# The last chunk of h turned by way of memory, in three stages of an encoder block

## The reference, cut to what matters

```python
h = h + 0.5 * swiglu(rmsnorm(h, ffn1_norm), ffn1_w_in, ffn1_w_out)
z = rmsnorm(h, mix_norm) @ w_mix_in
y = concat([rmsnorm(gating_unit(z), gnorm_a), rmsnorm(attention(z), gnorm_b)])
h = h + y @ w_mix_out
h = h + memory_cross_attention(rmsnorm(h, cross_norm), rmsnorm(mem, mem_norm), w_cq, w_ckv, w_co)
h = h + 0.5 * swiglu(rmsnorm(h, ffn2_norm), ffn2_w_in, ffn2_w_out)
out = rmsnorm(h, final_norm)
```

## Time and profile before

| | us |
|---|---|
| median of 3 runs (2161.65 to 2161.88) | 2161.73 |
| the profiled execution's own time | 2162.15 |
| its span | 2159.7 |
| PE (matmul) busy | 2149.6, 100% |
| DVE busy | 1167.4, 54% |
| ACT busy | 990.9, 46% |

### The profile page before, as it was taken

How to read it: one execution, slowest core, us unless ns; L and a number is a source line. 1 busy time by engine, 2 the same in 40 slices (tenths; PEclk the granted TensorE clock), 3 DMA queues, 4 the chain that set the end, 5 groups by cost and what they waited for, 6 DMA issues and landing times.

```text
span 2159.7 us, 26579 instructions
## 1 busy us (share of the span) xinstructions
PE 2149.6 (100%) x9544; PEld 1782.2 (83%) x9544; DVE 1167.4 (54%) x1158; ACT 990.9 (46%) x1133; POOL 46.2 (2%) x49
## 2 busy tenths in 40 slices
PE   9999999999999999999999999999999999999998
PEld 7888888888888888888888888888888888888887
DVE  5555555554555475556555644565555555554444
ACT  6444444443444455455444543454444444444443
POOL 0000000000000050000000000000000000000000
PEclk9999999999999999999999999999999999999999
DMA  8766676666666666765587765576666666765554
GB/s 302 248 218 212 213 225 218 213 214 193 217 224 213 244 230 218 246 216 172 173 288 236 230 205 185 183 226 210 213 225 218 213 214 222 220 213 193 193 186 155
DMA packets 179987, 466.05 MB, mean 216 GB/s; under 512 B 16721, under 2 KB 65105, under 8 KB 179793
## 3 DMA queue, kind: packets, MB, share of 16 engines
q1 hardware_dynamic: 177760, 457.90, 65.6%
q0 software_dynamic: 1728, 6.82, 0.9%
q10 hardware_dynamic: 432, 0.45, 0.1%
HBM read 438.36 MB, written 26.74 MB: 215 GB/s over the span
## 4 chain that ended last, share of the span: by engine, by line
PE 99%; DMA 1%; issue 0%; DVE 0%; ACT 0%; SPq 0%; POOL 0%; POOLq 0%; DVEq 0%; ACTq 0%
PE acc L1419 32%; PE acc L1421 32%; PE acc L1422 32%; PE acc L1517 1%; PE aux L1673 1%; PE aux L1653 1%; DMA bounce<-stage 0%; DMA memq<-bounce 0%; PE aux L1509 0%; PE aux L1610 0%; PE aux L1600 0%; PE aux L1573 0%; PE tp L1436 0%; PE acc L1496 0%; PE acc L1494 0%
## 5 line engine op out<-in xcount | busy, mean ns | idle before, releaser
L905 DVE TENSOR_TENSOR w_lo<-raw,w_hi 128x1024 fp32r<-128x1024 f32 x767 | 939.0, 1228 | 939.9 <-ACT w_hi L550 938.0
L550 ACT ACTIVATE w_hi<-raw 128x1024 fp32r<-128x1024 f32 x767 | 810.4, 1060 | 1092.1 <-PE acc L1422 1073.9
L1419 PE MATMUL acc<-w_hi,a_hi 128*128 128x512 f32 x1384 | 540.8, 391 | 0.0
L1422 PE MATMUL acc<-w_hi,a_lo 128*128 128x512 f32 x1384 | 539.3, 390 | 0.0
L1421 PE MATMUL acc<-w_lo,a_hi 128*128 128x512 f32 x1384 | 539.2, 390 | 0.0
L1419 PE MATMUL acc<-w_hi,b_hi 128*128 128x512 f32 x1216 | 476.5, 392 | 0.0
L1422 PE MATMUL acc<-w_hi,b_lo 128*128 128x512 f32 x1216 | 473.9, 390 | 0.0
L1421 PE MATMUL acc<-w_lo,b_hi 128*128 128x512 f32 x1216 | 473.9, 390 | 0.0
L1419 PEld LDWEIGHTS acc<-w_hi,a_hi 128*128 128x128 f32 x1384 | 260.0, 188 | 55.0 <-issue 1.3
L1422 PEld LDWEIGHTS acc<-w_hi,a_lo 128*128 128x128 f32 x1384 | 260.0, 188 | 53.8
L1421 PEld LDWEIGHTS acc<-w_lo,a_hi 128*128 128x128 f32 x1384 | 260.0, 188 | 53.3
(11 more groups left out here) (147 smaller groups left out, 623.9 us busy)
## 6 DMA issues: line engine op xcount, KB each, us to landing
raw<-in_ffn_w_in SPq DMA_DIRECT2D x351, 512.0 KB, 4.2
raw<-in_ffn_w_out SPq DMA_DIRECT2D x176, 512.0 KB, 4.3
raw<-in_w_mix_in SPq DMA_DIRECT2D x80, 512.0 KB, 4.3
raw<-in_w_ckv SPq DMA_DIRECT2D x64, 512.0 KB, 4.2
memq<-bounce SPq DMA_DIRECT2D x188, 128.0 KB, 3.7
bounce<-stage SPq DMA_DIRECT2D x37, 512.0 KB, 5.0
raw<-in_w_mix_out SPq DMA_DIRECT2D x32, 512.0 KB, 4.4
raw<-in_w_cq SPq DMA_DIRECT2D x32, 512.0 KB, 3.9
```

What stands on the lines that cost most here:

```text
L550: eng.activation(w_hi[:, u % RING], raw[:, u % RING], ACT.Copy).then_inc(w_hi_done, 1)
L905: eng.tensor_tensor(w_lo[:, u % RING], raw[:, u % RING], w_hi[:, u % RING].bitcast(f32), ALU.subtract).then_inc(w_lo_done, 1)
L1419: eng.matmul(dst, x_hi[:, rows], w_hi[:, slot, i], start=start and i == 0, stop=False)
L1422: last = eng.matmul(dst, x_lo[:, rows], w_hi[:, slot, i], start=False, stop=stop and i == UK - 1)
```

## The change

The last chunk of h goes by memory too, in all three places. PE's transposes, t_full, PE_FILLS, fill and fill_h are gone. SP sends the chunk ahead of load 7 of the next stage's first chunk and fetches it ahead of the second load of the chunk after (loads 7 and 8 stand between; the one that follows the fetch is load 9, counted from the first chunk's start). DVE turns it behind the split of unit 6 and subtracts behind that of unit 7; ACT's fill_hi stands behind its split of unit 7 and waits for the turn (turned) in place of t_full. mean_square comes ahead of the turn in all three. POOL's load_mem(0) waits for the new turn. On the host the rows of the last 512 of w_mix_in, w_cq, ffn2_w_in and the three gains are reordered as well.

```diff
@@ TURNS @@
-PE_FILLS = [("h1", 1), ("h2", 1), ("h3", 1)]
-TURNS = [("hid1", FJ), ("h1", DC - 1), ("qk", 4), ...
-         ("ck1", 1), ("yb1", 1), ("ck2", 1), ("ck3", 1), ("h2", DC - 1)] + ...
-         ("h3", DC - 1), ("hid2", FJ)]
+TURNS = [("hid1", FJ), ("h1", DC), ("qk", 4), ...
+         ("ck1", 1), ("yb1", 1), ("ck2", 1), ("ck3", 1), ("h2", DC)] + ...
+         ("h3", DC), ("hid2", FJ)]
@@ sync @@
-            def chunk(w, index, base, after_long=False, late=None, early=None, first=False):
+            def chunk(w, index, base, after_long=False, late=None, early=None, first=False, last=None,
+                      before=None):
                 for u in range(U8):
...
+                    if last and u == U8 - 1:
+                        send(*last)
+                    if before and u == 1:
+                        fetch(before[0])
                     load(w, index + u, base, u, after_long)
...
-                    chunk(w, 0, base, late=late)
-                    chunk(w, U8, base + U8)
+                    chunk(w, 0, base, late=late, last=last)
+                    chunk(w, U8, base + U8, before=last)
...
-                chunk(w_mix_in, U8 * c, MIX_IN + U8 * c, after_long=c == 0, late=late)
+                chunk(w_mix_in, U8 * c, MIX_IN + U8 * c, after_long=c == 0, late=late,
+                      last=from_h("h1", DC - 1) if c == 0 else None,
+                      before=from_h("h1", DC - 1) if c == 1 else None)
...
+                      last=from_h("h2", DC - 1) if c == 0 else None,
+                      before=from_h("h2", DC - 1) if c == 1 else None)
...
-            ffn_in(ffn2_w_in, FFN2_IN, "hid2", late=from_h("h3", DC - 2))
+            ffn_in(ffn2_w_in, FFN2_IN, "hid2", late=from_h("h3", DC - 2), last=from_h("h3", DC - 1))
@@ gpsimd @@
-            eng.wait_ge(turned, number(TURNS, "h1", DC - 2) + 1)
+            eng.wait_ge(turned, number(TURNS, "h1", DC - 1) + 1)
             load_mem(0)
@@ scalar @@
-                    if u == 6 and c == 0:
-                        fill_hi(t_full, number(PE_FILLS, "h1") + 1, a_hi[:, 3 * 4:4 * 4],
+                    if u == 7 and c == 0:
+                        fill_hi(turned, number(TURNS, "h1", 3) + 1, a_hi[:, 3 * 4:4 * 4],
                                 GAIN_AT["mix_norm"] + 3 * 4)
...
-                    if u == 6:
-                        fill_hi(t_full, number(PE_FILLS, "h3") + 1, b_hi[:, 12:16], GAIN_AT["ffn2_norm"] + 12)
+                    if u == 7:
+                        turned_h3_hi(DC - 1)
@@ vector @@
                     if u == 6 and c == 0:
                         mean_square("h1", DC, D)
+                        turn_fill("h1", DC - 1, number(TURNS, "h1", DC - 1))
+                    if u == 7 and c == 0:
                         fill_lo(split_number("h1", 3), a_lo[:, 12:16], a_hi[:, 12:16],
                                 GAIN_AT["mix_norm"] + 12)
...
                     if u == 6:
+                        mean_square("h3", DC, D)
+                        turn_fill("h3", DC - 1, number(TURNS, "h3", DC - 1))
+                    if u == 7:
                         fill_lo(split_number("h3", 3), b_lo[:, 12:16], b_hi[:, 12:16],
                                 GAIN_AT["ffn2_norm"] + 12)
-                        mean_square("h3", DC, D)
@@ tensor @@
-            def fill(srcs):
...
-                for k in range(4):
-                    for t in range(NT):
-                        last = eng.transpose(tp[:, k, t * P:(t + 1) * P], srcs(k, t), ident[:])
-                last.then_inc(t_full, 1)
...
-                    if u == 2 and c == 0:
-                        fill_h("h1", "h1", DC - 1)
...
-                    if u == 2 and c == 0:
-                        fill_h("h2", "h2", DC - 1)
...
-                    if u == 2:
-                        fill_h("h3", "h3", DC - 1)
```

More of the change, by code:

```diff
@@ L46 @@
          ("h2", DC), ("h3", DC), ("hid2", FJ)]
-PE_FILLS = [("h1", 1), ("h2", 1), ("h3", 1)]
-TURNS = [("hid1", FJ), ("h1", DC - 1), ("qk", 4), ("ya0", 1), ("ya1", 1), ("ck0", 1), ("yb0", 1),
-         ("ck1", 1), ("yb1", 1), ("ck2", 1), ("ck3", 1), ("h2", DC - 1)] + [(f"cq{k}", 1) for k in range(DC)] + [
-         ("h3", DC - 1), ("hid2", FJ)]
+TURNS = [("hid1", FJ), ("h1", DC), ("qk", 4), ("ya0", 1), ("ya1", 1), ("ck0", 1), ("yb0", 1),
+         ("ck1", 1), ("yb1", 1), ("ck2", 1), ("ck3", 1), ("h2", DC)] + [(f"cq{k}", 1) for k in range(DC)] + [
+         ("h3", DC), ("hid2", FJ)]
 AUX = ["sgu0", "sgu1"]
@@ L224, in encoder_block @@
         w_used = sem("w_used")
-        t_full = sem("t_full")
         sent = sem("sent")
@@ L347, in load_x, with ffn_in @@
                               ).then_inc(x_in[q], 16)
-            def ffn_in(w, base, hid, late=None):
+            def ffn_in(w, base, hid, late=None, last=None):
                 if base == FFN1_IN:
@@ L412, in _ @@
                 chunk(w_cq, U8 * c, CQ + U8 * c,
-                      late=from_h("h2", DC - 2) if c == 0 else queries(c - 2) if c >= 2 else None)
+                      late=from_h("h2", DC - 2) if c == 0 else queries(c - 2) if c >= 2 else None,
+                      last=from_h("h2", DC - 1) if c == 0 else None,
+                      before=from_h("h2", DC - 1) if c == 1 else None)
             for pos in range(DC * U8):
@@ L730, in _ @@
                                  sent, 16 * (number(TURNS, "qk", c - 6) + 1 if c > 5
-                                             else number(TURNS, "h1", 2) + 1))
+                                             else number(TURNS, "h1", 3) + 1))
                     if u == 4 and c == 0:
                         residual_squares("h1", DC - 1)
-                    if u == 6 and c == 0:
-                        fill_hi(t_full, number(PE_FILLS, "h1") + 1, a_hi[:, 3 * 4:4 * 4],
+                    if u == 7 and c == 0:
+                        fill_hi(turned, number(TURNS, "h1", 3) + 1, a_hi[:, 3 * 4:4 * 4],
                                 GAIN_AT["mix_norm"] + 3 * 4)
@@ L817, in _ @@
                         residual_squares("h2", DC - 1)
-                    if u == 6 and c == 0:
-                        fill_hi(t_full, number(PE_FILLS, "h2") + 1, b_hi[:, 3 * 4:4 * 4],
-                                GAIN_AT["cross_norm"] + 3 * 4)
+                    if u == 7 and c == 0:
+                        turned_h2_hi(DC - 1)
             def turned_h3_hi(k):
@@ L1315, in _ @@
                         mean_square("h2", DC, D)
-                        fill_lo(split_number("h2", 3), b_lo[:, 12:16], b_hi[:, 12:16],
-                                GAIN_AT["cross_norm"] + 12)
+                        turn_fill("h2", DC - 1, number(TURNS, "h2", DC - 1))
+                    if u == 7 and c == 0:
+                        turned_h2_lo(DC - 1)
             def turned_h3(c, u):
@@ L1498, in ffn_out @@
                     last.then_inc(last_ready, 1)
[L1500 to L1504, removed]
             eng.wait_ge(consts, 2)
@@ L1745, in lay_out @@
     turned = np.arange(CH).reshape(4, 4, 32).transpose(1, 0, 2).reshape(-1)
-    rows_of = {"ffn1_w_out": FJ, "ffn2_w_out": FJ, "w_mix_in": DC - 1, "w_cq": DC - 1,
-               "ffn2_w_in": DC - 1, "w_mix_out": DC,
-               "mix_norm": DC - 1, "cross_norm": DC - 1, "ffn2_norm": DC - 1, "gnorm_a": 2, "gnorm_b": 2}
+    rows_of = {"ffn1_w_out": FJ, "ffn2_w_out": FJ, "w_mix_in": DC, "w_cq": DC,
+               "ffn2_w_in": DC, "w_mix_out": DC,
+               "mix_norm": DC, "cross_norm": DC, "ffn2_norm": DC, "gnorm_a": 2, "gnorm_b": 2}
     cols_of = {"w_mix_in": MIX_COLS[4:8], "w_ckv": CKV_COLS[DC:], "w_cq": [CH * c for c in range(DC)]}
```

## The result

| | before | after |
|---|---|---|
| median, us (6 runs each) | 2161.81 | 2170.73 |
| lowest to highest | 2161.16 to 2162.18 | 2169.22 to 2172.30 |
| profiled execution | 2162.15 | 2172.30 |
| its span | 2159.7 | 2170.4 |

The ratio is 1.0041, with a 95% interval of 1.0031 to 1.0051: 8.9 us slower. The profiled execution is the slowest of the six.

What follows compares the result with a forecast made beforehand. PE's stream of matmuls was taken to bound the kernel (99% of the chain). Transposes removed, -2.64, plus PE stalls, +9.3, gave +6.7 us on the median of 2161.73: 2168.4 us, range 2164.2 to 2175.

Steps and rivals of the forecast that it cites:

- What is removed: Eight transposes on PE in each of three places, 0.88 us per fill, coming back in full: -2.64 us.
- The time that is free: From send issued to turn started before PE waits at unit 6: 5.8 us in h1, 7.9 in h2 and h3.
- the 4.69 us from the turn to t_read: End of the chain: from the turn's start to the end of DVE's subtraction takes 4.69 us, as at another turn of h.
- The round trip: Send issued to turn started: 11.1 us in h1, 9.9 in h2 and h3, stalling PE 5.3, 2.0 and 2.0 us.
- The sends: SP's 512 KB transfer of the chunk to memory, taken as 5.9 us in h1 and 4.7 in h2 and h3.
- the fetch: SP's fetch, first issue to turn started, taken as 5.2 us, with load 8 out some 3 us before the send landed.
- Rival A: The round trip is hidden in all three places: faster below 8.1 us, at best the whole gain, 2159.1 us; chance 0.06.
- Rival B: The array's clock falls in PE's stalls, about 1.9 us each: 2170.3 us for h1 alone, 2174.1 for all three; chance 0.14.
- 5.4 us of idle time as the limit: Clock falls over 5 us after PE stops, so h1's 5.3 us stall is about at the limit, the 2.0 far under.
- Rival C: Load 7 behind the send and load 9 behind the fetch slow the transfers: 2180.4 us, or 2172.3 with slow sends only; chance 0.14.
- Edits costed at nothing: Later load 7, load 9, weight splits on DVE and ACT, and POOL's mem loads stay inside the 5.5 us lead: 0 us.
- No other idle time on PE: Sign in the changed profile: PE waits only three times, ahead of unit 6, about 5 us in h1, 2 in h2 and h3.

Runs made afterwards that it cites:

- one_transpose: The kernel before with one of the eight PE transposes kept in each place, seven left out: 2159.58 us, -2.3 us to the kernel before.
- h23_only: The changed kernel with only h2 and h3 going by memory, h1 keeping PE's transposes: 2166.19 us, +4.3 us to the kernel before.
- fetch_first: The changed kernel with the fetch one load earlier on SP's queue, ahead of load 8: 2163.29 us, +1.5 us to the kernel before.
- bridge: The changed kernel with PE kept busy in its three waits by matmuls of ones: 2167.94 us, +6.1 us to the kernel before.
- early: The changed kernel with the last residual earlier on DVE in all three places, h1's send ahead of load 6: 2169.78 us, +7.9 us to the kernel before.

## Why the prediction was right, and where it was off

**Sign and size.** 2168.4 was forecast, 2170.73 measured, inside the range; +6.7 against +8.9 us.

**What is removed** (-2.64): right, as far as one_transpose can tell (-2.3 for seven of eight).

**The time that is free** (5.8, 7.9 and 7.9 us) and the 4.69 us from the turn to t_read: right. In h1 of the changed profile the turn starts at 741.46 and the subtraction ends at 744.35 + 1.66 = 746.01, 4.55 later; PE starts at 746.07.

**The round trip** (11.1, 9.9, 9.9): 11.1, 9.9 and 10.5 were measured, but by two errors that cancel, which is luck. The sends were 1.2 to 1.5 us shorter than taken: no row of a send from h before was under 3.9, and two came in at 3.2, with no other load issued in the 3.4 us before. The four rows behind the 4.7 all had a load issued at most 1.2 us ahead of the send; in this place the queue is quiet. The Trainium skill's formula (DMA: Bandwidth & Descriptors, section on the anatomy of one DMA) gives an estimate of 3.2 us for 512 KB; the page states it for transfers that GpSimd issues, and this send is SP's. The changed kernel's trace agrees with it in h2 and h3, at 3.2 us each; in h23_only, where no load had gone out for over 2.5 us either, the sends took 3.5 and 3.8. The step that failed is the fetch, the load ahead of the fetch "goes out some 3 us before the send has landed: I take 5.2". In h2 it went out at 1236.9, only 1.6 us ahead of the fetch, because the send was quick, and was still under way. 5.2 is what a fetch takes with load 8 behind it, as fetch_first shows (5.0 to 5.3).

**Rival A** (hidden): wrong for the changed kernel, and right for the places h2 and h3 once the load was out of the way: fetch_first's round trips there were 8.0 and 8.4 us, against the 7.9 that are free.

**Rival B** (the clock): it came true, in two of three places. The sum has no term for it, and this is the step that made it too small: the median is 2.2 us over the forecast, and the two falls cost 3.2 us in the profiled execution, which is 1.6 above the median. Rival B's own figure for one fall, 2170.3, is nearer to the 2170.73 than the forecast's 2168.4, whose range reaches over rival B and so held. I had 5.4 us of idle time as the limit, from the end of the kernel, and called h2's 2.0 us "far under". It fell there. The one row of before was one draw: in the profiles of this study the clock fell behind or in each of the five waits of 3.7 us or more in the three places, and of the nine shorter ones there in two (of 1.8 and 2.7 us) but not in those of 2.4 and 3.0. So a wait's length gives a chance of it, not a limit. Its price, about 1.9 us by the warm-up row, was 1.5 and 1.7 in the changed kernel and up to 2.6 (fetch_first). The Trainium skill (TensorE: Matmul & The Clock Gate, section on HAM oscillation) has waits for DMA put the array back to half rate; these runs agree where the clock fell, and bridge shows that filling the wait prevents it.

**Rival C** (transfers in each other's way): true as a mechanism, but its place was load 8 ahead of the fetch, not load 9 behind it, and its cost of 1.1 to 2.0 us in each place was about made good by the quick sends. Load 8 itself stands behind the fetch in fetch_first and does no harm there.

**Edits costed at nothing:** right in the three places, where PE waited for no weights. "No other idle time on PE" did not hold: the wait at the scores cost 1.2 us in the profiled execution, and its cause stays open. In h1 ACT waited 1.9 us for load 7, inside its lead; POOL's loads of mem went out at 743.3 and were there when ACT came to them.

## What to carry to other kernels

When a turn by memory replaces one in the array, count the time from producer to consumer before counting the array time saved: here 0.9 us saved stood against round trips of 10 us with 6 to 8 us free. In one in-order queue, put the latency-bound fetch ahead of the bulk load that is not yet needed; that order was worth 7 us here in three places and 6 in two. Starting the send earlier was worth 2.6 us in two places without that order and next to nothing on top of it, and in h1 of early, where three loads came to stand between send and fetch, PE's wait grew from 5.1 to 6.6 us. And a wait of a few microseconds in a dense stream of matmuls may cost another 1.5 to 2.6 us in the clock, or none.

## What the runs showed of the hardware that was not expected

The granted clock fell about 3 us after a wait of only 1.8 us had begun, when PE was already running again, and in another kernel held through one of 3.0. Useless matmuls in the waits kept it at its full level, and the kernel came out 2.8 us faster. A send of 512 KB to memory took 3.1 to 3.8 us behind a quiet queue and up to 6.0 elsewhere. A fetch of the same bytes took 4.5 to 5.6 us from its first issue to its turn with one load between send and fetch, 4.6 to 8.8 with two, and 10.6 with three. In h1 a slow send (6.0) went with a quick fetch (4.6) and a quicker send (4.1) with a slow one (7.4), as if the round trip as a whole waited for load 8 to drain; that was not tried by itself.
